# Row-tiled products, 64-wide value tiles and an early start in a chunked recurrence, and router logits moved behind the output projection

## The reference, cut to what matters

```python
def wkv7_scan(r, decay, k, v, a, b):            # 512 steps, 8 heads of 64 x 64 state
    def step(state, inp):
        r_t, w_t, k_t, v_t, a_t, b_t = inp
        sa = jnp.einsum('bhij,bhj->bhi', state, a_t)
        state = state * w_t[:, :, None, :] + sa[..., None] * b_t[:, :, None, :] + v_t[..., None] * k_t[:, :, None, :]
        y = jnp.einsum('bhij,bhj->bhi', state, r_t)
        return state, y
    ...

x = x + g1 * (mixed @ w_out)
h2 = rms_norm_2(x, norm2_g) * (1 + sc2) + sh2
scores = jax.nn.sigmoid(jnp.einsum('td,de->te', hf, router_w))     # hf = h2, 64 experts
...                                                                # top 4 groups, top 8 experts
shared = swiglu(hf, sh_gate, sh_up, sh_down)
```

## Time and profile before

| | |
|---|---|
| median of 3 runs | 2605.86 us (2601.21 to 2608.21) |
| profiled execution | 2612.11 us, span 2610.3 us |
| granted TensorE clock, mean | 0.947 |
| PE busy | 2359.9 us (90%), 8683 instructions |
| DVE, ACT, POOL busy | 896.1 (34%), 497.9 (19%), 401.0 us (15%) |
| phase_recur | 1435.7 to 1692.9 us of the span |
| phase_branches | 1693.0 to 1836.7 us |
| phase_route | 1836.8 to 1919.6 us |

### The profile page before, as it was taken

One profiled execution on the slowest core, in us unless ns is written; L12 is line 12 of the kernel. 1 busy time (PEld: TensorE's weight loads), 2 busy tenths in 40 slices (PEclk: granted clock), 3 DMA queues, 4 the chain that ended last, 5 costly groups with the idle time before them and its releaser, 6 DMA issues. The chain is left out here.

```text
span 2610.3 us, 23315 instructions
## 1 busy us (share of the span) xinstructions
PE 2359.9 (90%) x8683; PEld 1209.9 (46%) x8683; DVE 896.1 (34%) x1536; ACT 497.9 (19%) x929; POOL 401.0 (15%) x779
## 2 busy tenths in 40 slices
PE   6998988999999979999779898889769999999985
PEld 3443654443434434443343888834434444444432
DVE  3447832222220220007886233342541111111116
ACT  1013632111110010003244222200111111111121
POOL 0004000400000000000000100000034444444424
PEclk9999999999999989997789999999789999999997
DMA  8502004355333012213020950021149999899867
GB/s 349 213 21 105 1 1 166 113 190 193 105 105 135 2 66 79 82 48 97 25 83 29 402 215 1 13 114 51 64 193 380 387 403 364 352 411 394 339 262 285
DMA packets 68547, 446.29 MB, mean 171 GB/s; under 512 B 12228, under 2 KB 12884, under 8 KB 43506
## 3 DMA queue, kind: packets, MB, share of 16 engines
q0 software_dynamic: 36176, 254.42, 24.7%
q1 hardware_dynamic: 32290, 190.78, 19.1%
HBM read 416.27 MB, written 73.45 MB: 188 GB/s over the span
## 5 line engine op out<-in xcount | busy, mean ns | idle before, releaser
L2441 PE MATMUL psum<-arena 128*64 128x512 f32 (+1 forms) x1088 | 360.2, 594 | 0.0
L938 PE MATMUL psum<-arena 128*128 128x512 f32 x704 | 307.3, 596 | 3.2 <-PEq L870 3.2
L2441 PEld LDWEIGHTS psum<-arena 128*64 128x64 f32 (+1 forms) x1088 | 138.7, 164 | 185.0 <-issue 184.8
L938 PEld LDWEIGHTS psum<-arena 128*128 128x128 f32 x704 | 133.3, 191 | 177.4 <-issue 177.4
L2432 PE MATMUL psum<-arena 128*64 128x512 f32 (+1 forms) x544 | 186.2, 598 | 1.1 <-ACT arena L2474 1.1
L1176 PE MATMUL psum<-arena 128*128 128x512 f32 x384 | 166.9, 597 | 3.6 <-ACTq L1221 3.6
L1068 PE MATMUL psum<-arena 128*128 128x512 f32 x352 | 153.6, 598 | 7.0 <-PEq L157 7.0
L997 DVE SCALAR_TENSOR_TENSOR arena<-psum,arena 128x511 f32<-128x511 f32 x88 | 66.0, 750 | 253.2 <-ACT arena L972 251.6
L2502 DVE TENSOR_TENSOR arena<-arena,psum 128x256 f32<-128x256 f32 x51 | 21.5, 421 | 340.7 <-ACT arena L2470 340.7
L1784 PE MATMUL psum<-arena 128*128 128x128 f32 x1024 | 122.9, 280 | 7.8 <-DVE arena L1872 7.8
L1784 PEld LDWEIGHTS psum<-arena 128*128 128x128 f32 x1024 | 118.9, 194 | 11.5 <-DVE arena L1872 8.5
(11 more groups left out here) (493 smaller groups left out, 3060.0 us busy)
## 6 DMA issues: line engine op xcount, KB each, us to landing
scratch_expert_out<-arena SPq DMA_DIRECT2D x18, 2048.0 KB, 23.6
scratch_expert_out<-arena SPq DMA_DIRECT2D x51, 512.0 KB, 9.3
arena<-in_w_ada SPq DMA_DIRECT2D x12, 2048.0 KB, 16.8
arena<-in_ada_w POOLq DMA_DIRECT2D x12, 2048.0 KB, 8.2
arena<-in_w_up SPq DMA_DIRECT2D x22, 1024.0 KB, 5.0
arena<-in_w_in SPq DMA_DIRECT2D x9, 2048.0 KB, 8.0
arena<-in_w_down SPq DMA_DIRECT2D x5, 2048.0 KB, 8.1
arena<-in_w_o SPq DMA_DIRECT2D x2, 2048.0 KB, 8.4
```

The lines of the kernel that those rows point to most:

```text
L938: last = pe.matmul(K.bank[2 * (n % 3) + half], w[:, k, P * half:P * half + P], K.h[:, k, :], start=(k == 0), stop=(k == KD - 1))
L2441: last = pe.matmul(K.bank[2 + s][r, :], xt[:, s, P * k + r.start:P * k + r.stop], gu[:, lane, 2 * E_FF * k:2 * E_FF * (k + 1)], start=(k = ...
```

## The change

In the recurrence the products run on 64-row slices of `bk` and `ar`, one head each, instead of on `bkz`, which goes, with GpSimd's work for it; the two heads of a pair write different banks. The turned products now stand between the first and the second kind. The masks become 6 operations of 512 elements, 2 turned ones of 512 and 2 of 1024. x, u and y take 64 value columns a head. x, y without u, u, state, y with u is the new order. ScalarE copies half of x and u and the first part of y. The transposes and first products of the next chunk no longer wait for state and y.

In the branches phase the router's four small transfers are issued behind gate_r's, and the shared expert's two behind w_out's, ahead of the stores of h2. The logits of a token tile are made into that tile's PSUM after the next tile's turn. The route phase begins with exp, and its TensorE program waits for that exp.

```diff
-    bkz = K.ws[:, 0, 2048:4096].rearrange("p (h m t) -> p h m t", h=HEADS, m=2)
+    UNIT_BANKS, TURNED_BANKS, X_BANKS, U_BANKS, S_BANK, Y_BANKS = (3, 6, 0, 3), (5, 2), (0, 1), (2, 3), 5, (6, 7)
+    PRODUCTS = 6
 ...
+            def products(c, u, j, g):
+                for q in range(2):
+                    for h in range(2):
+                        rows = slice(64 * h, 64 * h + 64)
+                        last = pe.matmul(K.bank[UNIT_BANKS[u] + h][:, 256 * q:256 * q + 256], bk[rows, 2 * g + q, j, C * c:C * c + C],
+                                         ar[rows, 2 * g + q, :, C * c:C * c + C], start=True, stop=True)
+                pr_mm.by(last)
 ...
-                if c:
-                    pe.wait_ge(s_out.sem, c)
-                    pe.wait_ge(y_out.sem, 2 * c)
                 for j in range(3):
                     for q in range(4):
                         src = zv[:, q, now] if j == 2 else bk[:, q, j, now]
                         last = pe.transpose(K.bank[j][:, P * q:P * q + P], src, K.ident[:, :])
                     tr_pe.by(last)
-                pe.wait_ge(bz_in.sem, c + 1)
 ...
+                products(c, 0, 0, 0)
+                if c:
+                    pe.wait_ge(y2_out.sem, c)
+                products(c, 1, 0, 1)
+                if c:
+                    pe.wait_ge(s_out.sem, c)
+                pe.wait_ge(tr_out.sem, 3 * c + 3)
+                for q in range(4):
+                    for h in range(2):
+                        rows = slice(64 * h, 64 * h + 64)
+                        last = pe.matmul(K.bank[TURNED_BANKS[h]][:, C * q:C * q + C], ar[rows, q, 0, now], bk[rows, q, 0, now], start=True, stop=True)
+                pr_mm.by(last)
+                products(c, 2, 1, 0)
+                pe.wait_ge(pr_out.sem, PRODUCTS * c + 1)
+                products(c, 3, 1, 1)
+                pe.wait_ge(pr_out.sem, PRODUCTS * c + PRODUCTS)
 ...
                 for h in range(HEADS):
-                    q = h // 2
-                    out = K.psum[:, P * h:P * h + P]
-                    pe.matmul(out, mh[:, h, 0, :], tm[:, 2, P * q:P * q + P], start=True, stop=False)
-                    last = pe.matmul(out, ar[:, q, 0, now], state[:, q, :], start=False, stop=True)
-                x_mm.by(last)
+                    pe.matmul(half(X_BANKS, h), mh[:, h, 0, :], tm[:, 2, 64 * h:64 * h + 64], start=True, stop=False)
+                    last = pe.matmul(half(X_BANKS, h), ar[:, h // 2, 0, now], state[:, h // 2, 64 * (h % 2):64 * (h % 2) + 64], start=False, stop=True)
+                    if h % 4 == 3:
+                        x_mm.by(last)
 ...
+                for g in range(2):
+                    pe.wait_ge(x_out[g].sem, c + 1)
+                    for h in range(4 * g, 4 * g + 4):
+                        last = pe.matmul(half(U_BANKS, h), tt[:, h, :], xu[:, 0, 64 * h:64 * h + 64], start=True, stop=True)
+                    u_mm.by(last)
                 for q in range(4):
+                    if q % 2 == 0:
+                        pe.wait_ge(u_out[q // 2].sem, c + 1)
+                    out = K.bank[S_BANK][:, P * q:P * q + P]
 ...
                 s_mm.by(last)
+                pe.wait_ge(y_out.sem, c + 1)
+                for h in range(HEADS):
+                    last = pe.matmul(half(Y_BANKS, h), gb[:, h, :], xu[:, 1, 64 * h:64 * h + 64], start=True, stop=True)
+                y2_mm.by(last)
 ...
+                act.wait_ge(x_mm.sem, 2 * c + 2)
+                x_out[1].by(act.activation(xu[:, 0, 256:512], K.bank[X_BANKS[1]][:, 0:256], ACT.Copy))
+                act.wait_ge(y_mm.sem, c + 1)
+                y_out.by(act.activation(y(c).rearrange("p (b q) n -> p b q n", b=2), split(Y_BANKS[0]), ACT.Copy))
+                act.wait_ge(u_mm.sem, 2 * c + 2)
+                u_out[1].by(act.activation(xu[:, 1, 256:512], K.bank[U_BANKS[1]][:, 0:256], ACT.Copy))
 ...
+            def logits(t):
+                pe.wait_ge(moved.sem, t + 1)
+                for k in range(KD):
+                    last = pe.matmul(K.psum[:, D * t:D * t + EXPERTS], K.h[:, k, P * t:P * t + P], w_r[:, k, :], start=(k == 0), stop=(k == KD - 1))
+                lg_mm.by(last)
+
+            def after(t):
+                turn_rows(K, pe, K.h2, t, scaled, turned)
+                if t:
+                    logits(t - 1)
 ...
+            stream(K, sp, d["sh_gu"])
+            stream(K, sp, d["sh_down"])
 ...
             for t in range(NT):
                 sp.wait_ge(scaled.sem, t + 1)
                 h2_out.by(sp.dma_start(d["h2"][P * t:P * t + P, :], K.h2[:, t, :]), 16)
 ...
-            act.wait_ge(lg_mm.sem, 1)
-            expo.by(act.activation(sc[:, :, :].rearrange("p t e -> p (t e)"), K.bank[0][:, 0:NT * EXPERTS], ACT.Exp, scale=-1.0))
+            expo.by(act.activation(sc[:, :, :], K.psum[:, :].rearrange("p (t n) -> p t n", t=NT)[:, :, 0:EXPERTS], ACT.Exp, scale=-1.0))
```

More of the change, by code:

```diff
@@ L1796, in _ @@
-                x_mm.by(last)
-                for h in range(HEADS):
-                    q = h // 2
-                    out = K.psum[:, 1024 + P * h:1024 + P * h + P]
-                    pe.matmul(out, mh[:, h, 1, :], tm[:, 2, P * q:P * q + P], start=True, stop=False)
-                    pe.matmul(out, ar[:, q, 1, now], state[:, q, :], start=False, stop=True)
-                    if h == 0:
-                        pe.wait_ge(x_out.sem, 2 * c + 2)
-                    u = K.psum[:, 2048 + P * h:2048 + P * h + P]
-                    last = pe.matmul(u, tt[:, h, :], xu[:, 0, P * q:P * q + P], start=True, stop=True)
-                    if h == HEADS - 1:
-                        u_mm.by(last)
@@ L1808, in _ @@
-                pe.wait_ge(u_out.sem, 2 * c + 2)
-                for h in range(HEADS):
-                    q = h // 2
-                    last = pe.matmul(K.psum[:, 3072 + P * h:3072 + P * h + P], gb[:, h, :], xu[:, 1, P * q:P * q + P], start=True, stop=True)
-                y_mm.by(last)
+                    pe.matmul(half(X_BANKS, h), mh[:, h, 0, :], tm[:, 2, 64 * h:64 * h + 64], start=True, stop=False)
+                    last = pe.matmul(half(X_BANKS, h), ar[:, h // 2, 0, now], state[:, h // 2, 64 * (h % 2):64 * (h % 2) + 64], start=False, stop=True)
@@ new lines, in _ @@
+                    if h % 4 == 3:
+                        x_mm.by(last)
+                for h in range(HEADS):
+                    pe.matmul(half(Y_BANKS, h), mh[:, h, 1, :], tm[:, 2, 64 * h:64 * h + 64], start=True, stop=False)
+                    last = pe.matmul(half(Y_BANKS, h), ar[:, h // 2, 1, now], state[:, h // 2, 64 * (h % 2):64 * (h % 2) + 64], start=False, stop=True)
+                y_mm.by(last)
+                for g in range(2):
[3 more added lines that the diff above has]
+                    u_mm.by(last)
@@ L1880, in _ @@
                         else:
[L1881 removed]
+                            dve.wait_ge(pr_out.sem, PRODUCTS * c + PRODUCTS)
                         st_dve.by(dve.tensor_tensor(q, q, K.bank[(2 * i + g) % 8], ALU.add))
[L1884 to L1893 removed]
+                for mm, banks, to, out in ((x_mm, X_BANKS, xu[:, 0, 0:256], x_out), (u_mm, U_BANKS, xu[:, 1, 0:256], u_out)):
+                    dve.wait_ge(mm.sem, 2 * c + 1)
+                    out[0].by(dve.tensor_copy(to, K.bank[banks[0]][:, 0:256]))
                 dve.wait_ge(s_mm.sem, c + 1)
[L1895 removed]
+                new = K.bank[S_BANK].rearrange("p (q n) -> p q n", q=4)
                 for h in range(2):
@@ L1959, in _ @@
                 read(pe, n)
-            project_tokens(K, pe, sga, 2, 4, mm, lambda t: turn_rows(K, pe, K.h2, t, scaled, turned))
+            def logits(t):
[7 more added lines that the diff above has]
+                    logits(t - 1)
+            pe.wait_ge(router_in.sem, 64)
+            project_tokens(K, pe, sga, 2, 4, mm, after)
+            logits(NT - 1)
         @block.sync
@@ L2095, in _ @@
         def _(sp):
-            small.by(sp.dma_start(w_r[:, :, :], d["router_w"].rearrange("p (k e) -> p k e", e=EXPERTS)), 16)
-            small.by(sp.dma_start(bias[:, :], d["router_bias"].partition_broadcast(P)), 16)
-            small.by(sp.dma_start(const[:, :], d["route_const"]), 16)
-            small.by(sp.dma_start(tri[:, :], d["masks"][:, M_S, :]), 16)
-            stream(K, sp, d["sh_gu"])
-            stream(K, sp, d["sh_down"])
+            pass
         @block.tensor
         def _(pe):
-            pe.wait_ge(small.sem, 64)
-            for t in range(NT):
-                for k in range(KD):
-                    last = pe.matmul(K.bank[0][:, EXPERTS * t:EXPERTS * t + EXPERTS], K.h[:, k, P * t:P * t + P], w_r[:, k, :], start=(k == 0), stop=(k == KD - 1))
-            lg_mm.by(last)
+            pe.wait_ge(expo.sem, 1)
             w = take(K, pe).rearrange("p (k m) -> p k m", k=KD)
```

100 lines of the change are left out of this document (39 added, 61 removed).

## The result

| | before | after |
|---|---|---|
| median of 4 runs each | 2607.03 us (2601.21 to 2609.1) | 2572.68 us (2571.52 to 2578.01) |
| profiled execution | 2612.11 us, span 2610.3 | 2578.01 us, span 2576.2 |
| granted TensorE clock, mean | 0.947 | 0.948 |
| phase_recur | 1435.7 to 1693.0, 257.3 us | 1432.7 to 1666.6, 234.0 us |
| phase_branches | 1693.0 to 1836.7 | 1666.7 to 1821.0 |

The ratio of the timed runs is 0.9876, interval 0.9854 to 0.9897: 32 us less, between 27 and 38. Forecast were 20 us and a range of 2571 to 2601; the median lies 1.7 us inside its lower end. The direction and the places were right; the gain was undersized by 12 to 14 us, most of it in the recurrence.

A forecast was written before the change was run, and what follows sets the result against it. The prediction took TensorE's own work and standstills to bound the kernel. Recurrence 12.1 us plus router 8 us made 20 us, taken off the timed median 2605.9 for 2586 us; eight-in-ten range 2571 to 2601.

The forecast's parts named there:

- 1a: Each chunk's end, first x pass to last state pass: 96 passes in 10.7 us instead of 14.36; 14.6 us gained.
- 1b: From a chunk's last state pass to the next inverse: 13.8 us instead of 14.2, VectorE late next; 1.2 us gained.
- 1c: First chunk, until its inverse: 12.0 us instead of 19.65, no wait for GpSimd's zeroed copies; 7.6 us gained.
- 1d: Last chunk's end: y part with u and its addition now follow the state; 0.8 us lost.
- 1e: Recurrence clock: half clock at each inverse's start -8.8 us, two old falls replaced +3.3, one part-fall in narrow passes -5.
- part 1: All recurrence terms together: 12.1 us gained.
- Part 2: Router: logits made earlier and shared gate matmuls starting sooner; 8 us gained, bounds 4 and 13.
- rival 2: Recurrence: VectorE pays for the new access patterns and row halves don't overlap; 12 us, giving 2598; chance 0.12.
- Rival 1: Recurrence: clock falls in each chunk's 64-column passes, 13.8 us times four instead of 5, giving 2636; chance 0.09.
- 3: Router: stores behind the shared weights end the phase 4 us later than charged, giving 2590; chance 0.12.
- 4: Recurrence: narrow passes are cheaper, 80 of the 96 by half; 21 us in all, giving 2565; chance 0.04.
- 5: Whole kernel: nothing is left, several part-falls of the clock and dearer VectorE patterns together, 2600 to 2612; chance 0.05.

The follow-up runs named there:

- the wide kernel: Changed kernel with 128 moving columns again in 56 of the 64 passes of x and the first part of y per chunk; 2576.28 us, ratio 0.9875.
- kernel with the masks late: Changed kernel with only the VectorE work that the inverse's first step reads ahead of it, the rest behind, inverse banks reordered; 2558.23 us, ratio 0.9808.
- the filler: Changed kernel plus 18 matmuls that nothing reads, in TensorE's idle time ahead of each inverse; 2584.27 us, ratio 0.9904.
- the router's part alone: Kernel before with only the branches and router half of the diff, recurrence as before; 2600.58 us, ratio 0.9967.
- the last kernel: Changed kernel with less VectorE work ahead of the inverse, 128-column x, y, u and logits passes, later store wait, exp table loaded early; 2545.63 us, ratio 0.9767.

## Why the prediction came out as it did

By its own steps, in us gained, from the two profiled executions:

| step | forecast | measured | from |
|---|---|---|---|
| 1a chunk's end | 14.6 | 14.3 | 14.36 to 10.79, four times |
| 1b chunk to chunk | 1.2 | 4.4 | 14.2 to 12.72, three times |
| 1c first chunk | 7.6 | 8.6 | 19.65 to 11.07 |
| 1d last chunk | -0.8 | -0.5 | from behind the last state pass to the phase's end, 3.5 (1689.48 to 1692.98) to 4.04 (1662.61 to 1666.65) |
| 1e clock at the inverse | -8.8 | -6.8 | 32.69 to 34.32, 34.32, 34.3 and 34.6 |
| 1e falls replaced | +3.3 | +3.3 | before, second chunk: products 1.7 (turning to inverse 13.84, in the third chunk 12.17), inverse 1.6 (34.32, not 32.69) |
| 1e fall in narrow passes | -5 | 0 | clock 1.00 in all four |
| part 1 | 12.1 | 23.3 | 257.3 to 234.0; the rows above give 23.3 |
| part 2, with branches | 8 | 6.8 | 162.9 to 156.1, branches' start to gate matmuls |
| elsewhere | 0 | 4.0 | 3.1 ahead of the change |

**1a was right to 0.1 us a chunk**, with its unit: passes of 64 columns 0.11 us apart, as those of 128, shown by the wide kernel's same 10.79. All covers held: TensorE is busy for all of those 10.79 us.

**1b and 1c, VectorE's chain: mis-sized.** The step "6 masks at 0.67, 2 turned 1.3, 2 at twice 0.67, 2 additions 1.4, in all 9.4" took 8.3 (1493.16 to 1501.5; the groups 3.68, 1.28, 2.34 and 1.28 overlap at their ends). Four of the new masks last 2.48 (kernel with the masks late) where four old ones lasted 2.68, and the two of 1024 elements 2.34 where I took 2.7. Why the new access patterns are a little cheaper is open; rival 2 had it the other way round. "VectorE is late next" was right, with 4.96 us of idle time in place of 6.3, and the kernel with the masks late shows that it was all: 4.65 us earlier when 4.6 of VectorE's work went behind.
"Four microseconds that are cut from TensorE's products nobody waited for" is right too.

**1e, the clock.** That idle time brings it down at each inverse was right, and the filler and the late masks show it. It costs 1.6 a chunk three times and 1.9 once, not 2.2: the low stretches held 3.2 to 4.2 us of work, at the lower bound of what was charged. The charge of 5 for the narrow passes was the largest error of the sum. It did not occur in the changed kernel, yet such a fall exists: in two other kernels it took 8.1 us a time. The prediction added up two falls, of the idle time and of the narrow passes; in no chunk of any trace here do both stand. That the second would not come on top of the first was in no step of the prediction. Rival 1's objection ("there the low clock came from the idle time ahead") does not cover the filler's rows, where only 0.98 us idle lie near, as they do where the wide passes don't fall.

**Part 2.** 10.5 us are gained from the last turn to the gate matmuls. The forecast for that stretch was 9.8: its 9.5 count from a last turn that comes 1.8 later, so these 1.8 are to be added and the 1.5 of its two charges taken off. 3.8 us are lost ahead of the last turn: 2.2 between the projection's start and the last turn, where the first tile's logits (1.90) were put (forecast 1.8), and 1.6 ahead of the projection, where no instruction of TensorE is changed. Windows from the branches' start to the projection, before and after:

```profile
1693.03:1767.44 74.41, 61.17 (x145) 27.55 (x145) 33.78 (x40) 4.25 (x6) 1.62 (x3) 0.91 0.34 134
```

```profile
1666.69:1742.69 76.00, 62.96 (x144) 28.10 (x145) 33.67 (x40) 4.26 (x6) 1.61 (x3) 0.88 0.36 138
```

These 1.6 are clock: the same passes keep TensorE busy 1.8 us longer, at a mean clock of 0.88 in place of 0.91. They are no effect of the router's part. In the trace with the router's part alone the same stretch lasts 74.25 us, and from the branches' start to the gate matmuls it is 154.2 us against 162.8 before: 8.6 less, where 8 were forecast. Why the low stretches differ between executions is open. The stores ended the phase as said, 1.1 us late. What the Trainium skill says (DMA: Bandwidth & Descriptors, Queues, rings and completion order), named in the prediction, agrees with the trace: the two weights' transfers, issued first, land at 1811.8 and 1815.6, and the four stores, three of which were issued from 1804.70 on right behind them, one by one from 1816.9 to 1820.6, where SyncE's wait ends.

**Rivals.** 1 did not occur in the changed kernel. 2 (dearer access patterns) is out: the four-dimensional masks were cheaper than the old ones. 3 is out (1.1 us, as charged). 4 is out: 64 columns cost what 128 do. 5 is out with the time.

## What to carry to other kernels

When TensorE's work before a dependency is cut, read at once which engine ends last there: a cut of 4 us was worth nothing and even cost clock, and putting half of VectorE's work behind the first step that needs it was worth 18. The weight loads (PEld) were busy for all of the 10.79 us; there 64 moving columns saved nothing against 128, and could cost: reading along 64 unneeded columns was free and kept the clock up. A fall of the clock that one edit cures may hide another place that is next in line, so judge such an edit on the whole recurrence, over several executions.

## What was not expected of the hardware

- A stretch of 64-column float32 passes, 0.11 us apart and with no idle time among them, fell from full to half clock (at 1475.3 with the filler) and lasted 18.9 us instead of 10.8. It did so in three of eight chunks whose inverse had kept its clock and in none of twenty whose inverse had begun at half; with 128 columns none of twelve chunks fell.
- The stretch at half clock that begins ahead of the last turn ended under 128-column logits after 6.8 us (1776.6 to 1783.4 in the last kernel), but lasted 17.1 us (1809.0 to 1826.1) in the changed kernel, past all of its 64-column logits.
- Passes on the two 64-row halves run side by side even when all of one half is written before the other, and pass each other across matmuls of different lines (1435.99 before 1436.32).
- With identical instructions ahead, the recurrence began between 1427.3 and 1435.7 us in the profiled executions: 8 us of scatter that no change here makes.
